# Where tiles lie within 512 bytes of SBUF: one remainder for what the matmuls stream, one for the gate and up weights

## The reference, cut to what matters

```
D_MODEL, SEQ, D_FF, DEPTH_2 = 1024, 512, 2816, 2

def _swiglu(h, w_gate, w_up, w_down):
    return (jax.nn.silu(h @ w_gate) * (h @ w_up)) @ w_down

for layer in range(DEPTH_2):
    g = norm_gains[layer]
    x = x + 0.5 * _swiglu(_rmsnorm(x, g[0]), ffn_w_gate[layer, 0], ffn_w_up[layer, 0], ffn_w_down[layer, 0])
    h = _rmsnorm(x, g[1])
    mix = _conv_rwkv_mixer(h, ...) if layer % 2 == 0 else _mla_mixer(h, ...)
    x = x + mix.astype(x.dtype)
    x = x + 0.5 * _swiglu(_rmsnorm(x, g[2]), ffn_w_gate[layer, 1], ffn_w_up[layer, 1], ffn_w_down[layer, 1])
```

## Time and profile before

| | us |
|---|---|
| median of three runs | 2413.35 (2412.16 to 2414.78) |
| the profiled execution | 2413.27 |
| its span, first to last instruction | 2411.5 |
| PE busy in the span | 2339.2 (97%) |
| PEld busy | 1986.4 (82%) |
| DVE busy | 1738.6 (72%) |
| ACT busy | 1144.1 (47%) |
| POOL busy | 880.0 (36%) |

### The profile page before, as it was taken

One profiled execution on the slowest core, in us unless ns is written; L12 is line 12 of the kernel. 1 busy time (PEld: TensorE's weight loads), 2 busy tenths in 40 slices (PEclk: granted clock), 3 DMA queues, 4 the chain that ended last, 5 costly groups with the idle time before them and its releaser, 6 DMA issues.

```text
span 2411.5 us, 42260 instructions
## 1 busy us (share of the span) xinstructions
PE 2339.2 (97%) x16963; PEld 1986.4 (82%) x16963; DVE 1738.6 (72%) x2296; ACT 1144.1 (47%) x1758; POOL 880.0 (36%) x533
## 2 busy tenths in 40 slices
PE   8999989999999999988999999999999999999999
PEld 6667768789899777876898998998987557898997
DVE  7999986496486489765874867856856776883871
ACT  5533353465364346244662654643644344662552
POOL 3799944322313456422114133132134212114123
PEclk9999999999999999999999999999999999999999
DMA  5222214233343432002334343342333221233333
GB/s 151 79 79 79 75 57 127 74 88 100 104 115 90 111 90 74 27 3 58 111 95 118 106 114 89 88 131 77 114 88 100 52 58 53 81 101 107 106 89 96
DMA packets 420791, 214.48 MB, mean 89 GB/s; under 512 B 17317, under 2 KB 419035, under 8 KB 420603
## 3 DMA queue, kind: packets, MB, share of 16 engines
q1 hardware_dynamic: 416523, 209.05, 30.6%
q10 hardware_dynamic: 4080, 2.83, 0.5%
HBM read 209.22 MB, written 2.10 MB: 88 GB/s over the span
## 4 chain that ended last, share of the span: by engine, by line
PE 73%; DVE 17%; issue 3%; ACT 3%; POOL 3%; DMA 0%; ACTq 0%; DVEq 0%; POOLq 0%
PE bank L995 10%; PE bank L1000 10%; PE bank L1003 10%; PE bank L344 9%; PE bank L341 9%; PE bank L337 9%; DVE bank L1690 4%; PE bank L1863 2%; PE bank L1860 2%; PE bank L1856 2%; DVE gu_w_lo L592 1%; POOL w_lo L319 1%; PE bank L3400 1%; PE bank L2748 1%; DVE hL L368 1%
## 5 line engine op out<-in xcount | busy, mean ns | idle before, releaser
L319 POOL TENSOR_TENSOR w_lo<-w_raw,w_hi 128x1024 fp32r<-128x1024 f32 (+5 forms) x276 | 532.9, 1932 | 613.1 <-ACT w_hi L311 611.3
L311 ACT ACTIVATE w_hi<-w_raw 128x1024 fp32r<-128x1024 f32 (+5 forms) x276 | 237.6, 861 | 623.2 <-PE bank L344 468.7
L592 DVE TENSOR_TENSOR gu_w_lo<-gu_w,gu_w_hi 128x1024 fp32r<-128x1024 f32 (+1 forms) x256 | 364.9, 1428 | 90.6 <-ACT gu_w_hi L583 90.0
L664 POOL TENSOR_TENSOR ffn_aL<-tmp,ffn_aH 128x512 fp32r<-128x512 f32 x88 | 134.5, 1529 | 725.7 <-ACT ffn_aH L708 725.7
L583 ACT ACTIVATE gu_w_hi<-gu_w 128x1024 fp32r<-128x1024 f32 (+1 forms) x256 | 302.9, 1185 | 3.1 <-DVE gu_w L566 3.1
L995 PE MATMUL bank<-hH,gu_w_hi 128*128 128x256 f32 x1280 | 203.7, 281 | 5.0 <-ACT tmp L700 5.0
L1000 PE MATMUL bank<-hL,gu_w_hi 128*128 128x256 f32 x1280 | 200.7, 279 | 0.0
L1003 PE MATMUL bank<-hH,gu_w_lo 128*128 128x256 f32 x1280 | 200.3, 278 | 0.0
L700 ACT ACTIVATE tmp<-bank 128x256 f32<-128x256 f32 x320 | 120.8, 378 | 165.7 <-PE bank L1003 165.7
L968 DVE TENSOR_TENSOR bank<-bank,R 128x512 f32<-128x512 f32 x64 | 44.8, 699 | 204.1 <-PE bank L344 203.6
L337 PE MATMUL bank<-ffn_aH,w_hi 128*128 128x512 f32 x704 | 181.1, 390 | 0.0
(11 more groups left out here) (553 smaller groups left out, 4684.6 us busy)
## 6 DMA issues: line engine op xcount, KB each, us to landing
gu_w<-in_ffn_w_gate SPq DMA_DIRECT2D x88, 512.0 KB, 3.7
gu_w<-in_ffn_w_up SPq DMA_DIRECT2D x88, 512.0 KB, 4.8
w_raw<-in_w_in SPq DMA_DIRECT2D x48, 512.0 KB, 3.8
w_raw<-in_ffn_w_down SPq DMA_DIRECT2D x64, 384.0 KB, 3.4
w_raw<-in_ffn_w_down SPq DMA_DIRECT2D x64, 320.0 KB, 3.2
w_raw<-in_even_w_in SPq DMA_DIRECT2D x26, 512.0 KB, 3.9
w_raw<-in_w_conv_out SPq DMA_DIRECT2D x8, 512.0 KB, 3.9
w_raw<-in_w_out SPq DMA_DIRECT2D x8, 512.0 KB, 3.9
```

What stands on the lines that cost most here:

```text
L311: nc.scalar.activation(w_hi[u % 2][:, 0:K, :], w_raw[u % 4][:, 0:K, :], ACT.Identity).then_inc(w_hi_ready, 1)
L319: nc.gpsimd.tensor_tensor(w_lo[u % 2][:, 0:K, :], w_raw[u % 4][:, 0:K, :], w_hi[u % 2][:, 0:K, :].bitcast(F32), ALU.subtract).then_inc(w_l ...
L592: nc.vector.tensor_tensor(gu_wl[v % 3][:, b0:b1, :, :], gu_w[v % 3][:, b0:b1, :, :], gu_wh[v % 2][:, b0:b1, :, :].bitcast(F32), ALU.subtra ...
L664: nc.gpsimd.tensor_tensor(aL[:, in_half(n), :], up_t[:, :], aH[:, in_half(n), :].bitcast(F32), ALU.subtract).then_inc(a_lo, 1)
```

## The change

No instruction is added, taken away or moved on any engine; only the addresses of operands change. `place` works modulo 512 in all calls. The moving tiles start at 192 within 512 bytes, the gate and up weights at 128, except the buffer `gu_w0` (raw and low weights of units 0, 3, 6, 9 of a half), which starts at 192. To make room, the table of per-channel constants `par` goes in front, without the 248 columns of convolution taps; these get a tile `conv_w` of their own in block 1's part of memory, behind everything else there, and DVE writes and reads them there (L1608, and the taps at L1690).

Remainders of the start addresses modulo 512 (and, in brackets, modulo 256), worked out from the code:

| tile | before | after |
|---|---|---|
| `hH`, `hL`, `mixH`, `mixL`, `mH`, `mL` | 64 (64) | 192 (192) |
| `ffn_aH`, `ffn_aL` | 320 (64) | 192 (192) |
| `st_hi`, `st_lo`, `tmp`, `ident`, `ones` | 448 (192) | 192 (192) |
| `xT`, ring: `w_raw`, `w_hi`, `w_lo` | 320 (64) | 192 (192) |
| `gu_w_hi0` | 384 (128) | 128 (128) |
| `gu_w_hi1` | 0 (0) | 128 (128) |
| `gu_w0` = `gu_w_lo0` | 256 (0) | 192 (192) |
| `gu_w1` = `gu_w_lo1` | 384 (128) | 128 (128) |
| `gu_w2` = `gu_w_lo2` | 0 (0) | 128 (128) |

```
-            def place(self, r, step=256):
-
-                self.at += (r - self.at) % step
+            def place(self, r):
+
+                self.at += (r - self.at) % 512
                 return self.at
...
+        NPAR = 408
         m = Map(base0)
-        small = m.put("small", [P, 8])
-        m.place(64)
+        par = Map(m.at).put("par", [P, NPAR - TAPS * DT])
+        small = Map(m.at + 4 * (NPAR - TAPS * DT)).put("small", [P, 8])
+        m.at += 4 * (NPAR - TAPS * DT + 8)
+        m.place(192)
         xT = m.put("xT", [P, DT, T])
...
-        par = m.put("par", [P, 416])
...
-        hH_at = m.place(ring_at)
+        hH_at = m.at
         GU_PLACE = hH_at - 64
...
         f_map = Map(ARENA)
-        u_at = [f_map.place(GU_PLACE), 0, Map(ring_at).place(GU_PLACE)]
+        u_at = [f_map.at, 0, Map(ring_at).place(GU_PLACE)]
         f_map.put("gu_room0", [P, 7, 4, P])
...
-        u_at[1] = f_map.place(GU_PLACE, 128)
+        u_at[1] = f_map.place(GU_PLACE)
...
-        f_hi_at = f_map.place(hH_at, 128)
+        f_hi_at = f_map.place(hH_at)
...
+        conv_w = a.put("conv_w", [P, TAPS * DT])
...
-            V.tensor_scalar(par[:, cw_:cw_ + TAPS * DT], bank[2][:, cw_:cw_ + TAPS * DT], 0.5, None, M).then_inc(setup_rd, 1)
-            V.tensor_copy(par[:, cb_:cb_ + DT], bank[2][:, cb_:cb_ + DT]).then_inc(setup_rd, 1)
+            V.tensor_scalar(conv_w[:, :], bank[2][:, cw_:cw_ + TAPS * DT], 0.5, None, M).then_inc(setup_rd, 1)
+            V.tensor_copy(par_cols(cb_, cb_ + DT), bank[2][:, cb_:cb_ + DT]).then_inc(setup_rd, 1)
```

More of the change, by code:

```diff
@@ L160, in build, with par_cols @@
             cols(name, n)
-        NPAR = at
-        assert NPAR == 408
+        assert at == NPAR
+        def par_cols(a, b):
+            return par[:, a - TAPS * DT:b - TAPS * DT]
         def pc(name, j=0):
+            if name == "conv_w":
+                return conv_w[:, j:j + 1]
             c = COL[name] + j
-            return par[:, c:c + 1]
+            return par_cols(c, c + 1)
         def wview(ap):
@@ L373, in norm_tile_act @@
                 act.wait_ge(gu_done, all_done(GU_UNITS * (e + 1)))
-            high_tile(act, par[:, gcol + j:gcol + j + 1], j, new)
+            high_tile(act, par_cols(gcol + j, gcol + j + 1), j, new)
             square_tile(act, j, q)
         def norm_tile_dve(v, gcol, j, q):
-            low_tile(v, par[:, gcol + j:gcol + j + 1], j, q)
+            low_tile(v, par_cols(gcol + j, gcol + j + 1), j, q)
             sum_tile(v, j, q)
@@ L1549, in first_dve @@
             v.wait_ge(setup_ps, PRE_PS)
-            V.tensor_copy(par[:, pre_], bank[4][:, pre_]).then_inc(setup_rd, 1)
+            V.tensor_copy(par_cols(pre_.start, pre_.stop), bank[4][:, pre_]).then_inc(setup_rd, 1)
             for tt in range(TT):
@@ L1657, in first_dve @@
             v.wait_ge(setup_ps, PAR23_PS)
-            V.tensor_copy(par[:, pre_.stop:g_], bank[7][:, pre_.stop - 2 * P:g_ - 2 * P]).then_inc(setup_rd, 1)
-            V.tensor_scalar(par[:, g_:b_], bank[7][:, g_ - 2 * P:b_ - 2 * P], 0.5, None, M).then_inc(setup_rd, 1)
-            V.tensor_copy(par[:, b_:NPAR], bank[7][:, b_ - 2 * P:NPAR - 2 * P]).then_inc(setup_rd, 1)
+            V.tensor_copy(par_cols(pre_.stop, g_), bank[7][:, pre_.stop - 2 * P:g_ - 2 * P]).then_inc(setup_rd, 1)
+            V.tensor_scalar(par_cols(g_, b_), bank[7][:, g_ - 2 * P:b_ - 2 * P], 0.5, None, M).then_inc(setup_rd, 1)
+            V.tensor_copy(par_cols(b_, NPAR), bank[7][:, b_ - 2 * P:NPAR - 2 * P]).then_inc(setup_rd, 1)
             for c in range(2):
```

## The result

| | before | after |
|---|---|---|
| median of six runs, us | 2413.97 (2412.16 to 2416.85) | 2422.99 (2420.00 to 2424.87) |
| ratio, with its 95% interval | 1 | 1.0036 (1.0026 to 1.0046) |
| the profiled execution, us | 2413.27 | 2421.94 |
| its span, us | 2411.5 | 2420.1 |
| PE busy, us | 2339.2 | 2350.3 |

The forecast was 2407.5 us in a range up to 2416. The change makes the kernel slower by 0.36%, and the time lies above the range. It is the direction of rival B, and beyond its price.

The account below looks back on a forecast made before the run. PE's matmul spacing bounds the ends of halves, above a DVE and ACT floor of 9.77 us a unit. Savings 3.8 + 0.8 + 0.6 + 0.6 = 5.8 us off 2413.27 give 2407.5 us; 8-in-10 range 2404.5 to 2416.

Parts of the forecast that it names:

- rival B: Strassen units: a uniform layout keeps PE in the slow series; all slow costs 6.4 us, giving 2419.7 us; chance 0.15.
- The remainder modulo 256 is what counts: PE matmuls: series depend on start addresses modulo 256; two units differing only modulo 512 took 1.41 and 1.36 us alike.
- ring, tables, DVE and ACT zero: Ring keeps distance 0, and moved taps, `par` and `small` cost DVE, ACT and POOL nothing; each 0, ends +-1 us.
- Switches of the streamed tile end the fast series: Strassen units: four switches a unit between `hH`/`hL` and `st_hi`/`st_lo`, 320 in all, end 113.3 ns spacing; the change removes them.
- The fast series has no enemy left: Strassen units: only gaps and the low buffer at 192 still end 113.3 ns spacing; mean 115 ns, about 60% fast.
- 1930 of 1958, 0 of 180, 164 of 237: Matmuls staying fast in the old trace: with the same remainders, when the streamed tile switches, when only weights switch.
- The price of the mean: Strassen halves at 115 ns: 3.8 us for four second halves, 0.8 for the fourth FFN's first half, 0.6 for other first halves.
- floor of 9.77 us: Each Strassen unit: a loop of DVE and ACT, L851 to L851, limits what a faster PE can gain.
- The buffer at 192: `gu_w_lo0` at distance 0 in 4 units of 11: might end the fast series or leave PE slow.
- Plain units, 0.6 us: 384 matmuls, 512 wide: from 231.9 to 230 ns each at distance -64, saving 0.6 us; 2.0 if as the ring.
- The wait at P4 as an end of the fast series: Gap before product P4 in Strassen units: may settle the series anew or leave PE slow; no size of its own.
- rivals A and B: A, for Strassen units and ring: addresses change nothing that counts, 0 to -2 us, 2411 to 2413.5 us; chance 0.21.

Follow-up runs that it names:

- alt_w_st64: Changed kernel with `st_hi`/`st_lo` at 64 and gate/up weights taking turns at 128 and 0 (modulo 256), the old distances; 2412.37 us, 0.9998 of the kernel before.
- alt_w: Changed kernel with gate/up weights taking turns at 128 and 0 modulo 256, all streamed tiles at 192; 2405.92 us, ratio 0.9974 to the kernel before.
- dist0: Changed kernel with all five gate/up buffers at 192, distance 0 to everything streamed; 2434.12 us, ratio 1.0089 to the kernel before.
- lo_other: Changed kernel with high gate/up weights at distance -64 and low ones at +64 in every unit; 2417.60 us, ratio 1.0019 to the kernel before.
- lo0_128: Changed kernel with low buffer `gu_w0` at 128 like all other gate/up weights; 2421.15 us, ratio 1.0035 to the kernel before.
- plus64: Changed kernel with all five gate/up buffers at 256, distance +64 to everything streamed; 2418.02 us, ratio 1.0024 to the kernel before.
- dist128: Changed kernel with all five gate/up buffers at 320, distance 128 to everything streamed; 2432.66 us, ratio 1.0084 to the kernel before.

## Why the prediction was wrong, point by point

- **The remainder modulo 256 is what counts; ring, tables, DVE and ACT zero.** Right. `alt_w_st64` reproduces 107.70 us with every tile moved, the ring has its 1.36 us, DVE's busy time is 1738.6 us in both.
- **Switches of the streamed tile end the fast series.** Right. `alt_w` has none, and its share goes from 0.31 to between 0.72 and 0.90.
- **"The fast series has no enemy left", so the mean is 115 ns.** This is the step that failed. Every number behind it (1930 of 1958, 0 of 180, 164 of 237) is about leaving the fast series. The share of time in a series depends as much on how the slow one is left, and that was never counted. The count could have been made: in the trace of before a slow interval is followed by a fast one in 281 of some 4,020 cases, and 108 of them begin with the last matmul of a product, though 81 of these last a single interval. After, it is 8 of some 6,260, and all 8 are the last interval of a half, in front of the ring: inside the halves it is none. The change took away the enemy and the way back together. PE enters each half slow and nothing leads out: the mean was 117.98 ns where 115 stood.
- **The price of the mean.** The way it was worked out holds; that the figure fits so well is partly luck. The forecast had 0.95 us for a second half at 115 ns and 0.8 us for the fourth FFN's first half. `alt_w` gave 107.70 - 106.79 = 0.91 and 104.76 - 103.87 = 0.89. But `alt_w` ran at a mean of 113.75 ns in that half (waits left out), for which the prediction's own price was 1.1 (all fast). Of the missing 0.2, 0.16 is in the eight products from the last-but-one P4, which took 758.67 - 747.63 = 11.04 us with the wait in them, where 96 x 113.3 ns would be 10.88. The floor of 9.77 us and the end of a half were read well.
- **Rival B.** Its direction and its sentence "a uniform layout keeps whichever series is there" were right, and 0.15 was too low a chance for it. It was priced at 6.4 us and the halves lost 8.8. Of the difference of 2.4 us, 2.0 are in the second halves: the slow series is 117.7 to 117.8 ns rather than 117.5, which had been read from rows rounded to 0.01 us, and the passes at distance 0 take 119.7, which B had counted at 117.5 as well. 924 x (117.98 - 116.55) = 1.3 us a half, where B had 0.8. B's deciding point, a mean of 116.6 ns, is borne out: before stood at 116.55, and each layout above that is slower.
- **The buffer at 192.** The forecast let it stand as a small enemy of the fast series. It is a slower distance in its own right: 119.7 ns where it is one pass in three, 120.0 where it is everything, and no fast series (seven single intervals under 115 ns in all of `dist0`). It cost 0.19 us a second half.
- **Plain units, 0.6 us.** The size was right: 229.6 ns over 274 intervals at -64 against 231.9 before, 0.7 us for the 304 matmuls. It drowned in the 8.8.
- **The wait at P4 as an end of the fast series.** Named under rivals A and B, and missing from the sum. `lo_other` shows its weight: a layout that is fast until the first wait and has no way back is fast for a quarter of the half. Whoever is faster than the floor must have such waits, so the way back is needed in any layout that reaches the floor.
- **The rule on PE and SBUF.** The page "SBUF — State Buffer" of the Trainium skill says, in "Who interferes with whom", that PE never waits on anyone. Over kernels with the same instructions, a second half took from 106.76 to 110.89 us by addresses alone. The traces show no wait in these rows, but the rule can't be read as saying that addresses are free.

**Shown by the runs:** that the distances inside the units make the whole difference; that, where all streamed tiles are alike, a turn of the weights from -64 to +64 at the end of a product leads back and the same turn inside a product nearly never does; that the low buffer and the tables are not the cause. **Not settled:** why the place of the turn matters, and what inside the chip makes the series. No run here looks below the start times of the matmuls. That PE comes back behind a wait with high weights at +64 and mostly not at -64 is counted in these traces; no experiment varied the wait alone. In the kernel before, where the streamed tile switches too, the turn inside a product was often followed by a fast interval, nearly always a single one; that case is not sorted out here.

## What to carry to other kernels

When a quantity jumps between two steady states, count both directions before you price a change: what ends the good state and what ends the bad one. An edit that makes things uniform can remove the exits of both. And a layout that is only sometimes fast is worth trying in its parts: here the streamed tiles should be alike and the weights should not.

## What the runs showed of the hardware

- In these kernels the spacing of 128x256 float32r matmuls depends on the distance, modulo 256 bytes, between the start of what is streamed and the start of the weights: 113.3 or 117.7 to 117.8 ns at +-64 (`alt_w`, `lo0_128`, `plus64`), 120.0 at 0 (`dist0`), 118.7 or 120.0 at 128 (`dist128`). For 512 tokens it is another order: 226.7 to 227.3 ns at 0, 229.6 at -64 (kernel after), 233.3 at +64 (`plus64`), 232.7 at 128 (`dist128`).
- At +-64 the spacing has two steady series with the same addresses, clock and no wait. Which one holds depends on what came before, and the slow one can stay for the 924 matmuls of a half (`plus64`, `lo0_128`).
- The absolute address had no effect in the one pair of runs that tests it: `alt_w_st64` lies 128 bytes above the kernel before and has the same 107.70 us and 0.31. The ring kept its 1.36 us for six matmuls when its tiles moved from 64 to 192.
